# Feed-forward stage of a four-layer transformer step: the last iteration with both last rounds of outputs at its end, and token columns without padding

## What is computed

```python
for i in range(DEPTH):                      # DEPTH = 4
    sh1, sc1, g1, sh2, sc2, g2 = modulation(c, w_mod[i], b_mod[i])
    h = modulate(rmsnorm(x, norm1_g[i]), sh1, sc1)
    x = x + g1 * mixer_i(h)
    h = modulate(rmsnorm(x, norm2_g[i]), sh2, sc2)
    x = x + g2 * conv_ffn(h, ffn_w_in[i], ffn_conv_w[i], ffn_conv_b[i], ffn_w_out[i])
```

## Time and profile before

| | |
|---|---|
| time, median of 3 runs | 3270.67 us (3270.58 to 3274.07) |
| profiled execution: its time, its span | 3271.68 us, 3269.8 us |
| granted TensorE clock, mean | 0.967 |
| TensorE busy, share of the span | 94% |
| VectorE, ScalarE, GpSimd busy | 64%, 33%, 12% |
| chain that ended last | TensorE 89%, VectorE 6%, ScalarE 2% |

### The profile page before, as it was taken

How to read it: one execution, slowest core, us unless ns; L and a number is a source line. 1 busy time by engine, 2 the same in 40 slices (tenths; PEclk the granted TensorE clock), 3 DMA queues, 4 the chain that set the end, 5 groups by cost and what they waited for, 6 DMA issues and landing times.

```text
span 3269.8 us, 54337 instructions
## 1 busy us (share of the span) xinstructions
PE 3083.9 (94%) x21098; PEld 2813.1 (86%) x21098; DVE 2107.2 (64%) x4290; ACT 1071.4 (33%) x2074; POOL 403.9 (12%) x392
## 2 busy tenths in 40 slices
PE   8999999888999999998989899999989888999998
PEld 6899999766599999997865699999987668999998
DVE  7666666567756666656646566666666674766665
ACT  3222222326623222223335432222223563322221
POOL 3000000123310000003237310000012231000000
PEclk9999999889999999999988999999999899999999
DMA  8533323110023332330200223333321002122211
GB/s 336 198 116 128 115 97 113 54 55 1 22 95 129 120 124 91 114 116 31 78 30 6 93 78 116 112 120 117 127 73 52 4 1 91 65 78 77 67 62 45
DMA packets 47188, 289.96 MB, mean 89 GB/s; under 512 B 4945, under 2 KB 11345, under 8 KB 13265
## 3 DMA queue, kind: packets, MB, share of 16 engines
q1 hardware_dynamic: 47058, 288.21, 24.2%
HBM read 283.98 MB, written 4.21 MB: 88 GB/s over the span
## 4 chain that ended last, share of the span: by engine, by line
PE 89%; DVE 6%; ACT 2%; issue 1%; DMA 1%; POOL 0%; SPq 0%; POOLq 0%; DVEq 0%; ACTq 0%
PE psA L1945 39%; PE psB L1945 25%; PE psA L2046 3%; PE psA L2048 3%; PE psA L2047 3%; PE psB L1961 2%; PE psA L779 2%; PE psB L712 2%; PE psB L694 1%; PE psB L837 1%; PE psA L680 1%; DVE top L1671 1%; DVE top L1558 1%; DVE query L1514 1%; DMA m_stage<-w_mod_dram 1%
## 5 line engine op out<-in xcount | busy, mean ns | idle before, releaser
L1945 PE MATMUL psA<-h_hi,w_hi 128*128 128x322 f32 (+1 forms) x2848 | 661.2, 314 | 13.7 <-DVE h_lo L2378 13.7
L1945 PE MATMUL psA<-h_lo,w_hi 128*128 128x322 f32 (+1 forms) x2832 | 657.7, 313 | 0.0
L1945 PE MATMUL psA<-h_hi,w_lo 128*128 128x322 f32 x2816 | 648.4, 311 | 0.0
L2405 DVE SCALAR_TENSOR_TENSOR xT<-psB,mod,xT 128x128 f32<-128x128 f32 x1128 | 425.4, 433 | 249.8 <-PE psB L1945 249.8
L1945 PEld LDWEIGHTS psA<-h_hi,w_hi 128*128 128x128 f32 x2848 | 481.3, 190 | 17.1 <-issue 15.7
L1945 PEld LDWEIGHTS psA<-h_lo,w_hi 128*128 128x128 f32 x2832 | 482.7, 190 | 0.0
L1945 PEld LDWEIGHTS psA<-h_hi,w_lo 128*128 128x128 f32 x2816 | 480.1, 190 | 0.0
L2459 DVE TENSOR_SCALAR conv<-u_raw,vec_sb 128x642 f32<-128x642 f32 x176 | 108.3, 615 | 468.6 <-ACT u_raw L2244 468.6
L2244 ACT ACTIVATE u_raw<-psA 128x644 f32<-128x644 f32 x176 | 124.6, 708 | 741.2 <-PE psA L1945 741.2
L2290 DVE TENSOR_TENSOR w_lo<-w_stage,w_hi 128x512 fp32r<-128x512 f32 x496 | 345.9, 743 | 27.1 <-ACT w_hi L2163 27.0
L1945 PE MATMUL psB<-g_hi,wo_hi 128*128 128x322 f32 x1408 | 335.6, 320 | 23.7 <-DVE g_lo L2480 23.7
(11 more groups left out here) (257 smaller groups left out, 4526.3 us busy)
## 6 DMA issues: line engine op xcount, KB each, us to landing
w_stage<-weights_dram SPq DMA_DIRECT2D x124, 1024.0 KB, 4.9
m_stage<-w_mod_dram SPq DMA_DIRECT2D x96, 1024.0 KB, 8.3
wo_stage<-w_out_dram SPq DMA_DIRECT2D x44, 1024.0 KB, 4.8
yT_dram<-xT SPq DMA_DIRECT2D x8, 322.0 KB, 2.2
xT<-xT_dram SPq DMA_DIRECT2D x1, 1544.0 KB, 9.9
xT<-xT_dram SPq DMA_DIRECT2D x1, 1032.0 KB, 6.4
w_stage<-weights_dram SPq DMA_DIRECT2D x2, 512.0 KB, 17.8
rope_raw<-rope_dram SPq DMA_DIRECT2D x3, 256.0 KB, 2.7
```

The source lines that it names most:

```text
L1945: ins = pe.matmul(o, wp, xp[:, a:b], start=first and n == 0, stop=last and n == 2)
L2405: ins = dve.scalar_tensor_tensor(out=xT[:, d, c:c + w], in0=psB[:, bank, at_:at_ + w], scalar=gate[:, d, i:i + 1], in1=xT[:, d, c:c + w], ...
```

## The change

The token columns of `h_hi`, `h_lo`, `g_hi` and `g_lo` have no padding any more (`TOK` = 640), so the two halves of a product have 320 columns. They stand side by side at the border of two banks, the last 320 columns of one and the first 320 of the next. `tokens` reads the 128 context columns and the 512 latent columns, the latter across the border. `evac`, `gate` and the sum are two instructions each; the padding zeros are now set in `u_raw`, and the gated value has a buffer of its own, `gated`. The modulation's parts in psB move to the columns that are left free beside the pair.

The last iteration computes u tiles 0 to 3 and then the passes of iterations 9 and 10. Its g has buffers of its own, `g_hi_last` and `g_lo_last`. The output weights of iteration 10 are split in two halves of their output columns, the first after round 3 of pass 9, the second after round 7; pass 10 waits for each. Iteration 10's part of the modulation is computed ahead of rounds 6 and 7 of pass 9, into psA, and its transposes stand ahead of round 3 of pass 10. Loads are unchanged.

The diff, cut to its core (the many places where only `CTX0`, `LAT0` become 0, `SEQ` are left out):

```diff
@@ sizes and buffers
-HALF = COLS // 2
+TOK = SEQ + DEC_SEQ
+HALF = TOK // 2
...
+        g_hi_last = at("g_hi_last", [P, 2, TOK], F32R, B_NORM + 5 * C + 4 * (NT + 4) * P)
+        g_lo_last = at("g_lo_last", [P, 2, TOK], F32R, B_NORM + 3 * C)
+        gated = at("gated", [P, TOK], F32, B_NORM + 5 * C)
...
+        def tokens(ps, slot):
+            pair = ps[:, 2 * slot:2 * slot + 2, :].rearrange("p a n -> p (a n)")[:, BANK - HALF:BANK + HALF]
+            return pair[:, 0:SEQ], pair[:, SEQ:TOK]
+
+        def beside(g):
+            return [psB[:, 2 * g, 0:P], psB[:, 2 * g + 1, 3 * P:4 * P]]
@@ TensorE
             def halves(ps, slot):
-                return [(ps[:, 2 * slot + i, 0:HALF], (i * HALF, (i + 1) * HALF)) for i in range(2)]
+                return [(ps[:, 2 * slot, BANK - HALF:BANK], (0, HALF)), (ps[:, 2 * slot + 1, 0:HALF], (HALF, TOK))]
...
                 def out_pass(it, last=False):
+                    gh, gl = (g_hi_last, g_lo_last) if last else (g_hi, g_lo)
                     pe.wait_ge(s_g[l], it * 2 + 2)
-                    pe.wait_ge(s_wolo, it * 2 + (2 * ITERS * l + 2))
+                    if not last:
+                        pe.wait_ge(s_wolo, it * 2 + (2 * ITERS * l + 2))
                     for d in range(KT):
-                        if d == 0 and l < DEPTH - 1:
+                        if last and d % (KT // 2) == 0:
+                            pe.wait_ge(s_wolo, it * 2 + (2 * ITERS * l + 1 + d // (KT // 2)))
+                        if last and l < DEPTH - 1:
+                            if d == 3:
+                                mod_gap_sum(l, it)
+                            if d == KT - 1:
+                                pe.wait_ge(s_modok, it + (MOD_PASSES * (l + 1) + 1))
+                        if d == 0 and l < DEPTH - 1 and not last:
                             pe.wait_ge(s_modok, it + (MOD_PASSES * (l + 1) + 1))
...
                         if d >= KT - 2 and l < DEPTH - 1 and not last:
-                            mod_ffn(l, it + 1, d % 2)
+                            if isinstance(it, int) and it == ITERS - 2:
+                                pe.wait_ge(s_u[l], 4 * ITERS)
+                                mod_half(0, d % 2, it + (6 + MOD_PASSES * l + 2),
+                                         [psA[:, 2 * (d % 2) + c, 3 * P:4 * P] for c in range(2)])
+                            else:
+                                mod_ffn(l, it + 1, d % 2)
...
-                with pe.Fori(2, ITERS) as it:
+                with pe.Fori(2, ITERS - 1) as it:
                     ffn_iter(it, False)
+                for ft in range(4):
+                    u_tile(ITERS - 1, ft, False)
+                out_pass(ITERS - 2)
                 out_pass(ITERS - 1, True)
@@ ScalarE
-                    act.activation(u_raw[ft % 2][:, :].rearrange("p (a n) -> p a n", a=2),
-                                   psA[:, 2 * (ft % 2):2 * (ft % 2) + 2, 0:HALF], ACT.Copy).then_inc(s_u[l], 1)
+                    ctx, lat = tokens(psA, ft % 2)
+                    act.activation(u_raw[ft % 2][:, CTX0:CTX0 + SEQ], ctx, ACT.Copy)
+                    act.activation(u_raw[ft % 2][:, LAT0:LAT0 + DEC_SEQ], lat, ACT.Copy).then_inc(s_u[l], 1)
...
+                def ffn_last(it):
+                    for ft in range(4):
+                        evac(it, ft, False)
+                        if ft == 3:
+                            silu(it, 1)
+                        if l < DEPTH - 1:
+                            split_next(it, ft)
+                        if ft == 1:
+                            silu(it, 0)
+                            ghi(it, 0, g_hi_last)
+                    act.wait_ge(s_wo, it * 16 + 16 * (ITERS * l + 1))
+                    for half in range(2):
+                        act.wait_ge(s_o[l], it * KT - KT // 2 * (1 - half))
+                        c = slice(half * UNIT, (half + 1) * UNIT)
+                        act.activation(wo_hi[:, :, c], wo_stage[:, :, c], ACT.Copy).then_inc(s_wohi, 1)
+                        if half == 0:
+                            ghi(it, 1, g_hi_last)
@@ VectorE
-                for c, w, i in ((CTX0, SEQ, 0), (LAT0, HALF - LAT0, 1), (HALF, LAT0 + DEC_SEQ - HALF, 1)):
...
+                for i, (c, w) in enumerate(((CTX0, SEQ), (LAT0, DEC_SEQ))):
+                    ins = dve.scalar_tensor_tensor(out=xT[:, d, c:c + w], in0=tokens(psB, slot)[i],
...
+                for b in u_raw:
+                    own(dve.memset(b[:, 0:1], 0.0))
+                    own(dve.memset(b[:, LAT0 - 1:LAT0], 0.0))
+                    own(dve.memset(b[:, COLS - 2:COLS], 0.0))
...
-                    dve.tensor_tensor(conv[1][:, 1:COLS - 1], conv[0][:, 1:COLS - 1], conv[1][:, 1:COLS - 1],
-                                      ALU.mult).then_inc(s_gate[l], 1)
+                    for o, c, w in ((0, CTX0, SEQ), (SEQ, LAT0, DEC_SEQ)):
+                        ins = dve.tensor_tensor(gated[:, o:o + w], conv[0][:, c:c + w], conv[1][:, c:c + w], ALU.mult)
+                    ins.then_inc(s_gate[l], 1)
...
+                def ffn_last(it):
+                    more = l < DEPTH - 1
+                    for p in range(2):
+                        convolve(it, 2 * p)
+                        if more:
+                            lo_next(it, 2 * p)
+                        convolve(it, 2 * p + 1, (None, 0) if p else (None, None))
+                        if p:
+                            out_add(it - 1, 1)
+                        gate(it, p)
+                        if p:
+                            out_add(it - 1, 2)
+                            out_add(it - 1, 3)
+                        elif more:
+                            lo_next(it, 1)
+                        glo(it, p, g_hi_last, g_lo_last)
+                    for d in range(4, KT):
+                        out_add(it - 1, d)
+                        if d in (5, 7):
+                            half = d // 7
+                            c = slice(half * UNIT, (half + 1) * UNIT)
+                            dve.wait_ge(s_wohi, it * 2 + (2 * ITERS * l + half + 1))
+                            dve.tensor_tensor(wo_lo[:, :, c], wo_stage[:, :, c], wo_hi[:, :, c].bitcast(F32),
+                                              ALU.subtract).then_inc(s_wolo, 1)
+                    for d in range(KT):
+                        out_add(it, d)
+                        if d == 0 and more:
+                            mod_copy_ffn(l, it, 0, psA)
+                            mod_copy_ffn(l, it, 1, psA)
+                        if d == 2 and more:
+                            lo_next(it, 3)
+                        if d == 4 and more:
+                            mod_bias(l + 1, it, mod_parts(psA), it + (MOD_PASSES * (l + 1) + 1))
```

More of the change, by code:

```diff
@@ L166, in program @@
         conv = [at(f"conv{i}", [P, COLS], F32, B_N + M + (2 + i) * C) for i in range(2)]
-        g_hi = at("g_hi", [P, 2, COLS], F32R, B_N + M + 4 * C)
-        g_lo = at("g_lo", [P, 2, COLS], F32R, B_N + M + 6 * C)
+        g_hi = at("g_hi", [P, 2, TOK], F32R, B_N + M + 4 * C)
+        g_lo = at("g_lo", [P, 2, TOK], F32R, B_N + M + 6 * C)
         B_NORM = B_N + M + 8 * C
@@ L932, in out_ctx_hi @@
             def out_ctx_hi(g):
-                take(h_hi[:, 2 * g:2 * g + 2, CTX0:CTX0 + SEQ],
+                take(h_hi[:, 2 * g:2 * g + 2, 0:SEQ],
                      g_bank("o", g)[:, 0:2 * P].rearrange("p (a n) -> p a n", n=P), "o", g)
@@ L1983, in mod_ffn @@
                 mod_half(0, g, it + (6 + MOD_PASSES * l + 1),
-                         [psB[:, 2 * g + c, 3 * P:4 * P] for c in range(2)])
+                         beside(g))
             def mod_ffn_sum(l, it):
-                mod_sum(it * 2 + (MOD_PASSES * (2 * l + 1) + 2), [psB[:, c, 3 * P:] for c in range(4)])
+                mod_sum(it * 2 + (MOD_PASSES * (2 * l + 1) + 2), beside(0) + beside(1))
             def mod_gap(l, it):
@@ L2123, in out_pass @@
                                           (wo_hi[:, f, d * P:(d + 1) * P], wo_lo[:, f, d * P:(d + 1) * P]),
-                                          (g_hi[:, f, :], g_lo[:, f, :]), f == 0, f == 1)
+                                          (gh[:, f, :], gl[:, f, :]), f == 0, f == 1)
                         ins.then_inc(s_o[l], 1)
@@ L2295, in mod_bias @@
                 dve.wait_ge(s_mod, count)
-                own(dve.tensor_reduce(mod_sums[:, :, :], parts, AX_X, ALU.add))
+                sums = mod_sums[:, :, :]
+                if len(parts.shape) == 5:
+                    sums = sums.rearrange("p (a b) j -> p a b j", a=2)
+                own(dve.tensor_reduce(sums, parts, AX_X, ALU.add))
                 own.wait()
@@ L2413, in _ @@
             own(dve.memset(ones2[:, :], 1.0))
[L2414 removed]
             own(dve.memset(hits[:, :, :], 0.0))
[L2416 to L2419 removed]
+            dve.memset(ones[:, :], 1.0).then_inc(s_const, 1)
             own.wait()
@@ L2445, in _ @@
                     norm_dve(1)
-                for b in (g_hi, g_lo):
```

(16 more changed lines are left out.)

75 lines of the change are left out of this document (35 added, 40 removed).

## The result

| | before | after |
|---|---|---|
| time, median of 4 runs | 3272.37 us (3270.58 to 3274.96) | 3214.35 us (3212.77 to 3215.71) |
| ratio, 95% interval | | 0.9815 (0.9803 to 0.9828) |
| profiled execution: its time, its span | 3271.68, 3269.8 | 3212.77, 3211.0 |
| granted TensorE clock, mean | 0.967 | 0.969 |

What follows compares the result with a forecast made beforehand. TensorE, busy 94% of the span, was taken as the bound. Last iteration 29.6, columns 12.0, layer 3's waits 1.4 and shorter end sums 0.9 gave 43.9; 3271.7 less that and 1.0 made 3226.8 us, range 3217 to 3241.

Steps and rivals of the forecast that it cites:

- 320 columns for 322: All 13,824 products: two columns fewer save 0.865 ns each, 12.0 us; lower end 5.3, upper end 12.8.
- layer 3's waits: Layer 3's FFN: TensorE's nine waits for sums go, since sums get 0.13 us shorter; 1.4 us.
- Rival (a): Products at 322 columns: part is a fixed load of weights, columns give 5.3 instead of 12.0; 3233.5 us, chance 0.08.
- h's tiles start at other addresses ... I count zero: Products reading h, weights of the projections included: new start addresses change nothing, within 3 us either way.
- The last iteration: End of each layer: idle time 24.3 and slow clock 7.7 us go, less 2.4 of new stalls; 29.6 us.
- The chain through g_hi and g_lo: Pass 9: tile 3's chain ends at T+10.2, sum 4 at T+11.1, so round 6 loses 0.32 us.
- The second half of the next weight chunk waits ... zero: Pass 10: its load waits for the split after sum 2, near T+24, but is used much later; zero.
- rival (b): Passes 9 and 10 run by VectorE, 24 us of work in some 30; 19 us lost, 3246 us, chance 0.10.
- rival (c): Every pass: sums across two banks make each round wait, 56 us lost; slower, 3282 us, chance 0.04.
- m_stage: Pass 9, layers 0 to 2: load starts near T+17, lands at T+25, wanted near T+31; cover 6 us, zero.
- Eviction in two pieces: u tiles' eviction: at most 0.16 us more, covered by over 6 us before TensorE needs the slot; zero.
- The norm as long as before: Sign in the profile after: the norm between layers takes as long as before.

Runs made afterwards that it cites:

- the version from all this: Kernel after, with `w_lo` ahead, g_hi of tile 3 ahead of the wo_hi halves, and `g_hi`, `g_lo` at multiples of 512 bytes: 3201.47 us.
- the experiment: Kernel after with the old last iteration (u tiles 2 and 3 behind pass 9, pass 10 alone behind the wait for g_lo): 3246.6 us.

## Why the prediction was wrong in size

- **The term "320 columns for 322"** was mis-sized. I took a straight line from 322 to 512 columns, 0.865 ns for two columns, and held it for all 13,824 products; even its upper end (12.8 us) assumed a pace that scales with columns. In the steady iterations the u products gained 2.4 ns each; for all 8448 that is some 20 us where the term gave them 7.3. The first 288 of a layer gained less, 0.2 us in layers 1 and 2 and nothing in layer 3. The FFNs gave 24.0 us against 11.0 for columns and 1.4 for layer 3's waits. The runs put a step between 320 and 322 columns in its place, 2.3 to 3.3 ns with the price of the columns in it. A line through two rows can't show a step, and both of its rows were slowed by something else: 322 by the step, 512 by where h lay. Rival (a), columns cheap, erred the other way.
- **That the 4224 output products gained what the term said** was luck. The same 72 of them in layers 0 to 2, before, after and in the version from all this:

```profile
146.12 10.72 PE psB L1945 x72
```

```profile
144.71 10.65 PE psB L1960 x72
```

```profile
142.12 10.56 PE psB L1960 x72
```

  From 10.72 to 10.65 us is 0.97 ns each. With g laid anew it is 2.2 ns: a place of g that slows each sixth product hid the rest of the gain.
- **"h's tiles start at other addresses ... I count zero"** was wrong by 7.9 us: the starts of the 1440 products of 512 columns went from 232.3 to 226.9 ns in the mean, 7.8 us. The bound of 3 us had no row under it. "The trace shows no dependence" was true, and no evidence: in the kernel before, every product with h had the same spacing. The stretches themselves vary by 1 to 2 us between runs: together 355.3 to 357.9 us with h's tiles 2560 bytes apart, 361.3 to 365.3 with any other spacing.
- **The last iteration** was predicted at 29.6 us and gave 27.0 in the FFN stretches. Its main step held: the g_lo wait (24.2 us in the experiment) and the slow pass (16.64 against 14.2) went, and the passes run at a clock of 1.00. The chain through g_hi and g_lo ended 9.9 us after the pass began (10.2 predicted), and round 6 lost 0.4 us (0.32). In layer 3 the gain is 8.2 against my 7.4.
- **"The second half of the next weight chunk waits ... zero"** failed. I moved its load and forgot that the `w_lo` instructions now run beside GpSimd's squares; rival (b) priced the two at 1.3 us, and there they took 3.42. It cost 1.77 us in each of layers 0 to 2, 5.3 in all. With it given back, 27.0 would be 32.3. That step failed downward, so the sum hid part of the first two misses.
- **The sum of the misses.** By the spans it is 58.8 less 43.9, 14.9 us: 11.1 for the products and sums of the FFNs, 7.9 for where h lies, -2.6 for the last iteration, 1.2 for the clock in layer 0's first products, -0.8 for the output projections, -1.9 for attention, norms and start.
- **What held:** no sum is bound by the bank border (1.01 us; rival (c) out), passes 9 and 10 are not run by VectorE, but for the `w_lo` place in pass 10 (rival (b) out), layer 3's nine waits for sums are gone, and m_stage is loaded 15 us after the pass began, lands in 6.2 and is not waited for. Eviction in two pieces (0.28 and 0.60, overlapped) is covered.
- **"The norm as long as before"** was nearly so: +1.1 us in layers 1 to 3. Two norms were longer by 1.0 and 0.9 us in the ten products at L2023, 2.30 and 2.17 us for 1.28. The granted clock there was 0.50 and 0.55, and 1.00 or near it before, although TensorE had stood idle as long ahead of them (2.6 and 2.7 us in layer 1). In which norms it happens changes from run to run, so it is no effect of the edit.

## What to carry to other kernels

When an edit changes a product's width or where its operands lie, the slope between two other widths doesn't price it: read the pace of each form from starts, and widen the range by what a step of 1 to 3% in the pace would give, here 20 us. When an instruction is moved, ask not only who waits for it but what other engines do at its new place: VectorE instructions with two SBUF operands should not stand beside GpSimd's large ones. A stall covered in the steady loop must be counted again in the last iteration, where the next stage has already begun.

## What the hardware did that I had not expected

- With h's tiles 640 columns apart, u products of 320 columns start every 146.7 ns, that is 320 / 2.4 GHz and 13.3 ns, nearly without exception. With 656 or 672 (for `h_hi`) they are scattered by some ns and a little faster, 146.2 and 145.9 ns. In the kernel before, those of 322 start every 149.1 ns on average, scattered from 141 to 157. One half of 322 among halves of 320 costs 3.3 ns.
- Products of 512 columns with weights from h start every 226.7 ns when h's tiles and w lie at the same place modulo 512 bytes, and every 231 to 232 when h's tiles are 2576, 2624 or 2688 bytes apart. Output products that take 151 ns at the end of each f take 147 once g is laid so. But the place of their operands is not all of it: with only `h_hi` 672 apart it is the fifth of six that takes 151, and with h 656 apart the sixth, though g and the output weights lie at the same addresses in both and these products read no h. What unit counts, and whether it is the load of weights or the other operand, stays open, as does why 322 columns are worse.
- The Trainium skill (TensorE: Matmul & The Clock Gate, section Back-to-back issue gap) gives 2.5 ns over the columns for an isolated gap, and 131 ns at 512 columns for pairs of load and product. Both differ from the 13.3 ns and 226.7 ns here, and the measurement decides.
